# Third feed-forward: one 512-column moving operand for the gate and up units

## The reference

```
def swiglu_ffn(h, w_ffn_in, w_ffn_out):        # h (256 tokens, 1024)
    g, u = jnp.split(h @ w_ffn_in, 2, axis=-1)  # w_ffn_in (1024, 2*2816)
    return (jax.nn.silu(g) * u) @ w_ffn_out     # w_ffn_out (2816, 1024)

# in second_block, after the mixer:
h = rms_norm(x, ffn_pre_g[i]) * (1.0 + sc2) + sh2
y = swiglu_ffn(h, w_ffn_in[i], w_ffn_out[i])
x = x + g2 * rms_norm(y, ffn_post_g[i])
```

## Time and profile before

| | |
|---|---|
| median of 3 runs | 1211.08 us (1210.41 to 1212.88) |
| profiled execution | 1210.74 us, span of its instructions 1209.0 us |
| TensorE busy | 1152.7 us, 95% of the span |
| VectorE busy | 862.9 us, 71% |
| ScalarE busy | 622.2 us, 51% |
| HBM | 176 GB/s over the span |

### The profile page before, as it was taken

The page is one execution under the profiler, slowest core; times in us unless marked ns, Lnnn a source line. Parts: engine busy times, 40 slices in busy tenths (PEclk is TensorE's granted clock), DMA queues, the critical chain, the costliest instruction groups (busy, mean ns, idle before and its releaser), DMA issues.

```text
span 1209.0 us, 21217 instructions
## 1 busy us (share of the span) xinstructions
PE 1152.7 (95%) x8966; PEld 1115.6 (92%) x8966; DVE 862.9 (71%) x1404; ACT 622.2 (51%) x762; POOL 0.2 (0%) x4
## 2 busy tenths in 40 slices
PE   6999999999999999999999999999999989999996
PEld 5789899999999998998999999999988889999996
DVE  6996474777888779955757778887799757544543
ACT  7676336454434466753464544344587455443333
POOL 0000000000000000000000000000000000000000
PEclk9999999999999999999999999999999999999998
DMA  9555433656879555463336568795544332655511
GB/s 348 157 163 175 140 106 105 227 192 210 280 255 322 171 177 162 142 187 126 111 112 216 191 211 281 253 320 180 165 140 140 99 111 75 207 188 193 176 36 35
DMA packets 177615, 214.16 MB, mean 177 GB/s; under 512 B 3696, under 2 KB 160752, under 8 KB 177520
## 3 DMA queue, kind: packets, MB, share of 16 engines
q1 hardware_dynamic: 176800, 211.86, 53.4%
q10 hardware_dynamic: 720, 0.94, 0.2%
HBM read 211.74 MB, written 1.05 MB: 176 GB/s over the span
## 4 chain that ended last, share of the span: by engine, by line
PE 71%; DVE 19%; ACT 6%; issue 2%; DMA 1%; SPq 0%; DVEq 0%; ACTq 0%
PE stream L507 16%; PE stream L508 15%; PE stream L509 15%; DVE w_lo L1370 7%; PE steps L507 5%; PE steps L509 5%; PE steps L508 5%; PE steps L844 2%; ACT w_hi L928 2%; DVE conv_acc L1926 2%; PE steps L697 1%; PE stream L718 1%; DMA raw<-in_w_in 1%; ACT probs L928 1%; DVE h_norm L1450 1%
## 5 line engine op out<-in xcount | busy, mean ns | idle before, releaser
L1370 DVE TENSOR_TENSOR w_lo<-raw,w_hi 128x2048 fp32r<-128x2048 f32 (+2 forms) x178 | 401.4, 2266 | 205.3 <-ACT w_hi L928 203.7
L928 ACT ACTIVATE w_hi<-raw 128x2048 fp32r<-128x2048 f32 (+2 forms) x178 | 336.5, 1894 | 326.1 <-PE stream L509 294.2
L507 PE MATMUL stream<-h_hi,w_hi 128*128 128x256 f32 x1576 | 450.6, 286 | 12.1 <-DVE w_lo L1370 7.4
L509 PE MATMUL stream<-h_hi,w_lo 128*128 128x256 f32 x1576 | 446.5, 283 | 0.0
L508 PE MATMUL stream<-h_lo,w_hi 128*128 128x256 f32 x1576 | 446.5, 283 | 0.0
L507 PEld LDWEIGHTS stream<-h_hi,w_hi 128*128 128x128 f32 x1576 | 303.0, 192 | 16.3 <-DVE w_lo L1370 10.3
L508 PEld LDWEIGHTS stream<-h_lo,w_hi 128*128 128x128 f32 x1576 | 303.1, 192 | 0.5 <-issue 0.5
L509 PEld LDWEIGHTS stream<-h_hi,w_lo 128*128 128x128 f32 x1576 | 303.0, 192 | 0.0
L507 PE MATMUL steps<-gu_hi,w_hi 128*128 128x256 f32 x528 | 149.8, 284 | 1.4 <-DVE gu_lo L1665 1.4
L508 PE MATMUL steps<-gu_lo,w_hi 128*128 128x256 f32 x528 | 149.4, 283 | 0.0
L509 PE MATMUL steps<-gu_hi,w_lo 128*128 128x256 f32 x528 | 149.4, 283 | 0.0
(11 more groups left out here) (296 smaller groups left out, 1653.4 us busy)
## 6 DMA issues: line engine op xcount, KB each, us to landing
raw<-in_w_ffn_in SPq DMA_DIRECT2D x66, 1024.0 KB, 5.3
raw<-in_w_in SPq DMA_DIRECT2D x54, 1024.0 KB, 5.4
raw<-in_w_ffn_out SPq DMA_DIRECT2D x33, 1024.0 KB, 5.2
ada_raw<-in_ada_w SPq DMA_DIRECT2D x24, 1024.0 KB, 6.4
raw<-in_w_out SPq DMA_DIRECT2D x8, 1024.0 KB, 5.1
raw<-in_w_proj_attn SPq DMA_DIRECT2D x8, 512.0 KB, 3.5
raw<-in_w_proj_hgrn SPq DMA_DIRECT2D x8, 512.0 KB, 4.5
raw<-in_w_o SPq DMA_DIRECT2D x4, 1024.0 KB, 4.9
```

The lines of the kernel that those rows point to most:

```text
L507: pe.matmul(dst, w_h, x_h, start=start, stop=False, skip_group_check=True)
L509: return pe.matmul(dst, w_l, x_h, start=False, stop=stop, skip_group_check=True)
L928: return act.activation(out_, in_, func, **kw)
L1370: tt(wl[m % SPL][:, 0:n], raw[m % RAW][:, 0:n], wh[m % SPL][:, 0:n].bitcast(F32), ALU.subtract)\
```

## The change

In the third feed-forward the units gate and up of rounds 1 to 10 (`both_parts`, 20 units) are multiplied otherwise. The high and the low part of the input now lie side by side for each k (`h_both`, [P, KC, 2, T]; `hh` and `hl` are views of it). For each pair (n, k) TensorE issues one matmul of 512 columns, high weights x (high | low), into a whole bank, and one of 256 columns, low weights x high, into the first half of that bank. So there are two matmuls and two weight loads for each pair where there were three, and the same number of columns. Output n has bank n of the unit: each such unit has two banks.

On the way out the halves of each bank are added: ScalarE copies the two second halves to SBUF (`second_parts`, into `sg` for a gate and `gu` for an up unit), then VectorE adds the first halves to them (`add_parts`). ScalarE's silu then works in place in SBUF, for which it waits for the add; the product into gu follows the adds of the up unit. ScalarE's split of the unit three ahead stands behind the copies instead of ahead of the evacuation. Gates of these rounds are counted as evacuated by VectorE. The bank plan follows from the same code:

```diff
--- before.py
+++ after.py
@@ -137,6 +137,10 @@
     return u[1] == 2 and (u[2] in ("gate0", "val0") or u[0] in ("gate", "up") and u[2] == 0)
 
 
+def both_parts(u):
+    return u[0] in ("gate", "up") and u[1] == 2 and u[2] > 0
+
+
 def first_half(u):
     return u[0] == "tw" and u[2][-1] == "0"
 
@@ -146,7 +150,7 @@
     kind, b, name = u[:3]
     if kind == "up":
         return "gu"
-    if kind == "merge" or (kind == "out" and b < 2) or (kind == "gate" and scaled_after(u)) or name in ("val0", "val1", "f") or shifted(u):
+    if kind == "merge" or (kind == "out" and b < 2) or (kind == "gate" and (scaled_after(u) or both_parts(u))) or name in ("val0", "val1", "f") or shifted(u):
         return "dve"
     return None if kind == "down" or first_half(u) else "act"
 
@@ -167,7 +171,7 @@
             for x in banks:
                 last[x] = (e, count[e])
         elif e or first_half(u):
-            for _ in range(2 if u[0] in ("merge", "tw") or shifted(u) else 1):
+            for _ in range(2 if u[0] in ("merge", "tw") or shifted(u) or both_parts(u) else 1):
                 if bank == 3 and u[0] in ("gate", "up") and u[1] < 2:
                     bank = 0
                 banks.append(bank)
@@ -181,6 +185,7 @@
 
 
 BANKS, MOD_FREE = plan_banks()
+BOTH_GATES = [u[1:3] for u in UNITS if u[0] == "gate" and both_parts(u)]
 
 
 def build(nc, a, out):
@@ -194,8 +199,8 @@
     wh = [at(f"w_hi{i}", [P, 2048], F32R, 48 + 8 * i) for i in range(SPL)]
     wl = [at(f"w_lo{i}", [P, 2048], F32R, 72 + 8 * i) for i in range(SPL)]
     xT = at("xT", [P, KC, T], F32, 96)
-    hh = at("h_hi", [P, KC, T], F32R, 104)
-    hl = at("h_lo", [P, KC, T], F32R, 112)
+    h_both = at("h_hi_and_lo", [P, KC, 2, T], F32R, 104)
+    hh, hl = h_both[:, :, 0, :], h_both[:, :, 1, :]
     hn = at("h_norm", [P, KC, T], F32, 120)
     rel = at("rel", [P, IH, T], F32, 120)
     ytm = at("y_tm", [P, NT, 512], F32, 120)
@@ -362,6 +367,7 @@
     p_sq, p_ms, p_rs = Event("post_squares", 4), Event("post_sum"), Event("post_rstd")
     x_hi, x_lo, n_rt, rt_set = Event("x_gained_hi", 4), Event("x_gained_lo", 4), Event("rstd_turned"), Event("rstd_of_token_set")
     sg_silu, d_part = Event("gate_silu_set", 2), Event("down_part", 3)
+    both_silu, both_copied = sem("both_gate_silu_set"), sem("both_second_parts_copied")
     x_new = Event("x_updated", 4)
     y_copied = Event("y2_copied", 4)
     x2_new = Event("x2_updated", 4)
@@ -583,6 +589,14 @@
                 elif kind == "merge":
                     for half in range(2):
                         mm = merge_half(m, half)
+                elif both_parts(UNITS[m]):
+                    for n, k in in_order(2, KC):
+                        ready(k)
+                        ws = (slice(None), k, slice(P * n, P * n + P))
+                        pe.matmul(bank(m, n), hi[ws], h_both[:, k].rearrange("p i t -> p (i t)"), start=k == 0,
+                                  stop=False, skip_group_check=True)
+                        mm = pe.matmul(bank(m, n)[:, 0:T], lo[ws], hh[:, k, :], start=False, stop=k == KC - 1,
+                                       skip_group_check=True)
                 elif kind == "down":
                     ready(0)
                     g_h, g_l = gu_h[name % 2], gu_l[name % 2]
@@ -1045,6 +1059,13 @@
             f(ya_h[:, :, P * qt:P * qt + P], src, ACT.Copy).then_inc(*lane.mark(a_hi))
             yield
 
+        def second_parts(dst):
+
+            unit_in()
+            for n in range(2):
+                ins = f(dst[:, T * n:T * n + T], bank(here(), n)[:, T:2 * T], ACT.Copy)
+                ins.then_inc(*((both_copied, 1) if n else lane.step()))
+
         def feed_forward(b):
             if b < 2:
                 f(ones_r, ones, ACT.Copy).then_inc(*lane.mark(ones_rounded))
@@ -1052,7 +1073,13 @@
                 rstd(rs, A[0][:, 0:T], D, n_ms.at(5), n_rs, load=False)
                 normed_hi(5)
             for i in range(FS):
-                tick()
+                step()
+                both = both_parts(UNITS[here()])
+                if both:
+                    if i >= 2:
+                        act.wait_ge(*f_gu.at(b, i - 2))
+                else:
+                    split_ahead()
                 if shifted(UNITS[here()]):
                     shifted_in(sg[i].rearrange("p (c t) -> p c t", c=2), here(), ACT.Silu, g_silu)
                 elif scaled_after(UNITS[here()]):
@@ -1062,12 +1089,21 @@
                     f(sg[i % 2], sg[i % 2], ACT.Silu).then_inc(*lane.mark(sg_silu))
                     if i == 0:
                         normed_hi(2 * b + 1)
+                elif both:
+                    second_parts(sg[i % 2])
+                    split_ahead()
+                    act.wait_ge(*evacuated(here()))
+                    f(sg[i % 2], sg[i % 2], ACT.Silu).then_inc(both_silu, 1)
                 else:
                     unit_in()
                     if i >= 2:
                         act.wait_ge(*f_gu.at(b, i - 2))
                     f(sg[i % 2], bank(here()), ACT.Silu).then_inc(*emptied())
-                tick()
+                step()
+                if both:
+                    act.wait_ge(*f_lo.at(b, i - 1))
+                    second_parts(gu)
+                split_ahead()
                 act.wait_ge(*f_gu.at(b, i))
                 if i >= 2:
                     act.wait_ge(unit_done, UFF[b] + 3 * (i - 2) + 5)
@@ -1249,7 +1285,7 @@
             for j in range(4):
                 tick()
                 act.wait_ge(*g_mix.at(b, j))
-                f(hh[:, 2 * j:2 * j + 2, :].rearrange("p c t -> p (c t)"), mixa[j % 2], ACT.Copy).then_inc(*lane.mark(g_hi))
+                f(hh[:, 2 * j:2 * j + 2, :], mixa[j % 2].rearrange("p (c t) -> p c t", c=2), ACT.Copy).then_inc(*lane.mark(g_hi))
             for j in range(4):
                 step()
                 act.wait_ge(*evacuated(UOUT[b] + j))
@@ -1433,6 +1469,17 @@
             tt(dst, bank(here()).rearrange("p (c t) -> p c t", c=2), rs.unsqueeze(1).broadcast_to([P, 2, T]), ALU.mult)\
                 .then_inc(*emptied())
 
+        def add_parts(dst):
+
+            dve.wait_ge(both_copied, 2 * BOTH_GATES.index(UNITS[here()][1:3]) + 1 + (UNITS[here()][0] == "up"))
+            for n in range(2):
+                part = dst[:, T * n:T * n + T]
+                ins = tt(part, bank(here(), n)[:, 0:T], part, ALU.add)
+                if n == 0 or UNITS[here()][0] == "up":
+                    ins.then_inc(*lane.step())
+                else:
+                    ins.then_inc(*emptied())
+
         def normalise(ni, g, shift=None):
 
             def low(j):
@@ -1626,6 +1673,9 @@
                 step()
                 late = scaled_after(UNITS[here()])
                 shift = shifted(UNITS[here()])
+                both = both_parts(UNITS[here()])
+                if both:
+                    add_parts(sg[i % 2])
                 if shift:
                     dve.wait_ge(*n_rs.at(5))
                     shifted_evac(sg[i].rearrange("p (c t) -> p c t", c=2), 0, True)
@@ -1643,7 +1693,7 @@
                     s3 = sg[i % 2].rearrange("p (c t) -> p c t", c=2)
                     tt(s3, s3, rs.unsqueeze(1).broadcast_to([P, 2, T]), ALU.mult).then_inc(*lane.step())
                     dve.wait_ge(*lane.last)
-                elif not shift:
+                elif not shift and not both:
                     dve.wait_ge(evac["act"], BANKS[here() - 1][2])
                 unit_in()
                 if i:
@@ -1657,6 +1707,11 @@
                     for c in range(2):
                         ins = stt(g3[:, c, :], g3[:, c, :], sbias[:, 1, c:c + 1], sg[i][:, T * c:T * c + T], ALU.add, ALU.mult)
                         ins.then_inc(*(lane.mark(f_gu) if c else lane.step()))
+                elif both:
+                    add_parts(gu)
+                    dve.wait_ge(*lane.last)
+                    dve.wait_ge(both_silu, BOTH_GATES.index((b, i)) + 1)
+                    tt(gu, gu, sg[i % 2], ALU.mult).then_inc(*lane.mark(f_gu))
                 else:
                     tt(gu, bank(here()), sg[i % 2], ALU.mult).then_inc(*lane.mark(f_gu))
                 dve.wait_ge(*f_hi.at(b, i))
@@ -1796,8 +1851,8 @@
                 dve.wait_ge(*lane.last)
                 tt(mixa[j % 2], mixa[j % 2], mixb, ALU.add).then_inc(*lane.mark(g_mix))
                 dve.wait_ge(*g_hi.at(b, j))
-                tt(hl[:, gs, :].rearrange("p c t -> p (c t)"), mixa[j % 2],
-                          hh[:, gs, :].rearrange("p c t -> p (c t)").bitcast(F32), ALU.subtract).then_inc(*lane.mark(g_lo))
+                tt(hl[:, gs, :], mixa[j % 2].rearrange("p (c t) -> p c t", c=2), hh[:, gs, :].bitcast(F32), ALU.subtract)\
+                    .then_inc(*lane.mark(g_lo))
                 split_ahead()
             for j in range(4):
                 step()

```

## The result

The changed kernel takes 1215.41 us (median of 11 executions, 1213.57 to 1217.77) against 1211.08 us. The ratio is 1.0036 with a 95% interval of 1.0027 to 1.0044: **slower by 0.36%, 4.3 us**. The forecast was 1213.9 us, slower: the direction is right, and the loss is 1.5 us larger than forecast. The profiled execution is the slowest of the eleven, 1217.77 us with a span of 1216.0; before, it was 1210.74 and 1209.0. So I compare stages, not spans.

A forecast was written before the change was run, and what follows sets the result against it. TensorE was taken to bound the kernel, busy in all 167.10 us of the stage. 1210.74 + 4.2 (bank) - 3.74 (matmuls) + 2.35 (clock) = 1213.55, plus 0.34 to the median: 1213.9 us; range 1211.2 to 1215.5.

The forecast's parts named there:

- The bank: Up 1 needs up 0's banks, so it waits for up 0's evacuation and product until about 1027.3: +4.2 us.
- The clock: TensorE's 6.5 us idle ahead of up 1 brings half clock after the restart: +2.35 us (1.6 to 3.1).
- Rival 1: Bank wait ahead of up 1 at full clock, only 4.2 - 3.74: 1211.5 us, chance 0.08.
- The matmuls: Pairs in 18 gate and up units from gate 2 on take 347 instead of 360 ns: -3.74 us.
- rival 3: Gate and up pairs gain less or nothing (1217.6 us without gain), or a stall comes in every round; chance 0.1.
- Rival 2: Columns alone set the pace of gate and up pairs: 321 ns, net -4.7 us, 1206.4 us; chance 0.08.
- signs of being wrong: Gap under 4 us, clock staying at 1.00, pair pace not 347 ns, or TensorE waiting at gate/up from i = 2.
- At nothing: Added copies, adds and moved split fit, 6.6 us within 11.3 us of cover; interleaving costs nothing, bounds -0.3 and +0.3 us.
- Sum: Whole kernel, against the profiled execution: 1210.74 + 4.2 - 3.74 + 2.35 = 1213.55 us, +2.8; as median 1213.9 us.
- The range: Whole kernel's time from 1211.2 to 1215.5 us, covering full clock up to the whole half-clock stretch and a few tenths.
- likeliest case: Whole kernel's time from 1212.7 to 1214.8 us, depending on how long the half clock lasts.

The follow-up runs named there:

- run 4: The changed kernel with 46 extra 256-column matmuls, whose result nobody reads, issued in the gap ahead of up 1: 1213.34 us, ratio 1.0022 to the kernel before.
- Run 2: The kernel before, three matmuls a pair, with two banks reserved for each gate and up unit of the third feed-forward: 1216.11 us, ratio 1.0050.
- run 1: The changed kernel with the new form only from round 2 on, so up 1 has one bank again: 1208.95 us, ratio 0.9985 to the kernel before.

## Why the prediction was right, step by step

- **The bank.** Up 1 waits for f_gu(2, 0), at the place and through the queue foretold. The forecast was +4.2 us; run 4, which keeps the wait and takes the idleness away, has +4.22 in that stretch. Run 2 shows that it comes from the plan alone.
- **The clock.** Forecast +2.35 us (1.6 to 3.1), from two stretches of the trace of before. Measured 2.43 us in the profiled execution (20.47 - 18.04) and 1.7 between the changed kernel and run 4 by their ratios. That the fall comes, and roughly what it costs, was foreseen; that 5.27 us of it lay behind the restart, next to the 5.1 assumed, is luck, since in run 2 it was 3.2 us, at a cost of about 1.4. Rival 1, the wait without the clock, is refuted.
- **The matmuls: the mis-sized term.** The step failed that took "both at their own pace, 227 + 120 = 347 ns". In turn they take 353 ns (over all their starts in the stretch, 236.5 from a 512-column start to the next and 116.8 from a 256-column one), so that a pair gains 7 ns and not 13, and the 18 units 1.99 us and not 3.74. The sum was bounded wrongly: its other end lay below 347, at 321, and a dearer pair stood only in rival 3. Rival 2 (columns alone, 321 ns) is refuted; rival 3 was right in its first half, a smaller gain, at about half of its price (1.75 us of the gain lost, not all 3.74). "The pair's pace is not 347 ns" is also one of the prediction's own signs of being wrong, and it came; its other signs did not.
- **At nothing.** The copies, adds and the moved split fit: no wait of TensorE on a gate or up unit from round 2 on, and run 1, with 18 of the 20 evacuations, is faster than before. ScalarE's two copies took 0.66 us together, less than the 0.94 that I had from the earlier trace rows:

```profile
1066.53 0.66 ACT L942 ACTIVATE silu_g<-stream 128x256 f32<-128x256 f32 x2 [2.76 <-PE stream L598]
```

- **Sum.** 4.22 + 2.43 - 1.99 = +4.66 us by stages, +4.33 measured, against +2.8 forecast; the difference by stages, 1.85 us, is the pace of the pair but for 0.1. The range held the median with 0.1 us to spare, which is luck too. The "likeliest case" was also not what its sum gives: with 1.6 to 3.1 us of clock it runs from 1213.1 to 1214.6, not from 1212.7.

Two things stay open. Why the next start comes 9 ns later behind a 512-column matmul when 256-column ones lie between, and why five such matmuls pass before the pace is 227 ns, was measured but not traced to a cause. One idea, that the weight load has less time to hide behind a 256-column matmul, was not tried. And of the fall in gaps of 2.7 us only the mean over executions is known.

## What to carry to other kernels

A form that takes twice the PSUM banks halves the rotation, and the price is not paid where all rounds are alike but at the one place where the order has no other unit in between: write down, for every unit, which evacuation its bank waits for, and look there first. A wait of TensorE can be dearer than its length: here it cost 4.2 us at full clock and 2.4 us more by the clock (1.4 in run 2), so a change worth 7 ns a pair was lost in one wait. The paces of two kinds of matmul, each read among its own kind, do not add up to the pace of the two in turn.

## What the runs showed of the hardware that I had not expected

- Matmuls of 512 and 256 columns in turn: 353 ns a pair; grouped by eight: 349; the sum of the two paces of the kernel before: 347. In a group of eight the first five 512-column ones take 228 to 236 ns, the last three 227.
- A gap of 2.74 us from start to start went with more time at half clock: 24.0 us on average against 20.4 with the gap filled, and 1.2 us by the ratios, whose intervals overlap. The clock fell at 226 us, just behind an idle stretch of 1.9 us that both kernels have, in the changed kernel's profile and not in that of before.
- A filled gap is no waste: 46 matmuls whose result nobody reads took 2.4 us out of the stage, 1.7 us by the ratios.
